# Key tiles of the second block's attention: two heads in one tile, 64-row scores, meta parts multiplied together

## The reference

```python
# windowed attention: 16 query heads, 4 key heads of 64; 256 keys under a mask, 16 meta keys, a sink
s_band = where(mask, q @ k.T * 64 ** -0.5, -1e30)
s_meta = q @ k_meta.T * 64 ** -0.5
p = softmax(concat([s_band, s_meta, sink]))
o = p_band @ v + p_meta @ v_meta
# differential attention: 8 heads, two key and query parts of 64 each, values of 128, all 272 keys
p = softmax(q_c @ k_c.T * 64 ** -0.5)          # c = 0, 1
o = rms_norm((p_0 - lam * p_1) @ v) * (1 - lambda_init)
```

## Time and profile before

| what | value |
|---|---|
| median of 3 runs | 981.12 us |
| lowest, highest | 980.5, 982.21 us |
| span of the profiled execution (its own time, first to last instruction) | 978.5 us |
| mean granted TensorE clock in it | 0.990 |
| PE busy | 952.4 us (97%) |
| weight loads busy | 846.0 us (86%) |
| DVE, ACT, POOL busy | 591.6, 451.9, 47.2 us |

### The profile page before, as it was taken

One profiled execution on the slowest core, in us unless ns is written; L12 is line 12 of the kernel. 1 busy time (PEld: TensorE's weight loads), 2 busy tenths in 40 slices (PEclk: granted clock), 3 DMA queues, 4 the chain that ended last, 5 costly groups with the idle time before them and its releaser, 6 DMA issues.

```text
span 978.5 us, 15576 instructions
## 1 busy us (share of the span) xinstructions
PE 952.4 (97%) x6056; PEld 846.0 (86%) x6056; DVE 591.6 (60%) x1088; ACT 451.9 (46%) x752; POOL 47.2 (5%) x92
## 2 busy tenths in 40 slices
PE   6999999999999999979999999999999899999997
PEld 4888999987999999857778889999999699999996
DVE  5666765566545544577745776577766664554454
ACT  6535535345544344344444454556543454434432
POOL 0000010000000000020000000022230100000000
PEclk7999999999999999989999999999999999999999
DMA  9653334553555454513332212222245355545531
GB/s 349 245 213 134 125 130 172 173 206 130 209 178 201 176 177 157 181 44 129 150 137 101 86 45 86 87 87 87 92 160 223 130 176 192 191 171 184 201 130 44
DMA packets 21541, 148.94 MB, mean 152 GB/s; under 512 B 2528, under 2 KB 2784, under 8 KB 3952
## 3 DMA queue, kind: packets, MB, share of 16 engines
q1 hardware_dynamic: 20592, 145.52, 41.8%
q10 hardware_dynamic: 896, 2.69, 0.8%
HBM read 147.15 MB, written 1.05 MB: 151 GB/s over the span
## 4 chain that ended last, share of the span: by engine, by line
PE 93%; DVE 3%; ACT 1%; POOL 1%; issue 1%; DMA 1%; POOLq 0%; SPq 0%; ACTq 0%; DVEq 0%
PE ps L385 26%; PE ps L386 26%; PE ps L387 26%; PE ps L1252 3%; PE ps L1203 2%; PE ps L1223 2%; PE ps L1205 1%; PE ps L1254 1%; PE ps L394 1%; DVE xT_l L1366 1%; PE ps L1209 1%; PE ps L1210 1%; PE ps L397 1%; PE ps L961 1%; POOL stat L902 1%; DVE xn L1359 1%
## 5 line engine op out<-in xcount | busy, mean ns | idle before, releaser
L1345 DVE TENSOR_TENSOR wlo<-raw,whi 128x2048 fp32r<-128x2048 f32 x135 | 308.8, 2290 | 216.4 <-ACT whi L510 216.1
L510 ACT ACTIVATE whi<-raw 128x2048 fp32r<-128x2048 f32 x135 | 258.2, 1917 | 243.8 <-PE ps L387 232.5
L385 PE MATMUL ps<-xT_h,whi 128*128 128x256 f32 x864 | 246.5, 285 | 1.5 <-DVE xT_l L1366 1.5
L386 PE MATMUL ps<-xT_l,whi 128*128 128x256 f32 x864 | 244.4, 283 | 0.0
L387 PE MATMUL ps<-xT_h,wlo 128*128 128x256 f32 x864 | 244.3, 283 | 0.0
L385 PEld LDWEIGHTS ps<-xT_h,whi 128*128 128x128 f32 x864 | 165.5, 192 | 2.6 <-issue 1.9
L386 PEld LDWEIGHTS ps<-xT_l,whi 128*128 128x128 f32 x864 | 165.5, 192 | 0.6
L387 PEld LDWEIGHTS ps<-xT_h,wlo 128*128 128x128 f32 x864 | 165.5, 192 | 0.0
L385 PE MATMUL ps<-whi,xT_h 128*128 128x512 f32 (+1 forms) x336 | 133.8, 398 | 3.1 <-DVE xT_l L1366 3.1
L387 PE MATMUL ps<-whi,xT_l 128*128 128x512 f32 (+1 forms) x336 | 130.8, 389 | 0.0
L386 PE MATMUL ps<-wlo,xT_h 128*128 128x512 f32 (+1 forms) x336 | 130.7, 389 | 0.0
(11 more groups left out here) (296 smaller groups left out, 1392.4 us busy)
## 6 DMA issues: line engine op xcount, KB each, us to landing
raw<-weights SPq DMA_DIRECT2D x135, 1024.0 KB, 4.8
cst<-consts SPq DMA_DIRECT2D x1, 1571.0 KB, 13.5
h<-x_tiles SPq DMA_DIRECT2D x2, 512.0 KB, 5.5
raw<-weights SPq DMA_DIRECT2D x2, 512.0 KB, 6.7
gain_rows<-gain_rows ACTq DMA_DIRECT2D x1, 1024.0 KB, 7.1
y<-h ACTq DMA_DIRECT2D x4, 256.0 KB, 2.3
gain_row<-gain_rows ACTq DMA_DIRECT2D x1, 512.0 KB, 3.8
row<-rows SPq DMA_DIRECT2D x1, 144.0 KB, 14.4
```

The source lines that it names most:

```text
L385: pe.matmul(o, lh, rh, start=first, stop=False)
L386: pe.matmul(o, lh, rl, start=False, stop=False)
L510: act.activation(whi[s][:], raw[s][:], ACT.Copy).then_inc(split_hi, 1)
L1345: dve.tensor_tensor(wlo[s][:], raw[s][:], whi[s][:], ALU.subtract).then_inc(split_lo, 1)
```

## The change

Keys: `ksT` and `kbT` hold the two heads of a pair on partitions 0 to 63 and 64 to 127 of one tile, without zeros; ACT writes them with fewer copies (for `kbT` one of 128 partitions in place of two of 64; for `ksT` three per pair in place of two). In `ksT` the second head's keys stand with the 16 meta keys first. Scores: one product per head over all 272 keys, from the 64 rows of that head, into bank 4 (first head) and bank 5 (second). DVE takes one reduction of 272 per head; the maximum over two parts goes, and the constants gain 48 columns of zeros around the mask. The probabilities of both heads lie in one tile so that their meta parts are 16 columns, a gap of 16 zeros, and 16 columns; one transpose turns both. The meta values become tiles of 128 partitions, zero but for partitions 0 to 15 and 32 to 47, and one 128-row product opens the accumulation for both heads. POOL clears these value tiles, the gaps and `pmT`, and no longer the key tiles.

```diff
-        kbT = new("kbT", [P, 2 * F_HEADS, KEYS])
-        ksT = new("ksT", [P, S_KV, KEYS])
-        vs_meta = new("vs_meta", [N_META, S_KV * DH])
+        kbT = new("kbT", [P, F_HEADS, KEYS])
+        ksT = new("ksT", [P, S_KV // 2, KEYS])
+        vs_meta = new("vs_meta", [P, S_KV * DH])
...
-        sc = [new("sc0", [P, 2, KEYS]), new("sc1", [P, 2, KEYS])]
+        sc = [new("sc0", [P, SECOND + KEYS]), new("sc1", [P, SECOND + KEYS])]    # SECOND = 256 + 32
...
-        pmT = new("pmT", [N_META, 2, P])
+        pmT = new("pmT", [P, P])
...
-                        ins = copy_halves(*((ksT, 2 * cc) if r == 0 else (kbT, 4 * (r - 1) + 2 * cc)), 4 + cc)
+                        if r == 0:
+                            act.activation(ksT[0:DH, cc, :], ps[0:DH, 4 + cc, 0:KEYS], ACT.Copy)
+                            act.activation(ksT[DH:P, cc, N_META:KEYS], ps[DH:P, 4 + cc, 0:TOK], ACT.Copy)
+                            ins = act.activation(ksT[DH:P, cc, 0:N_META], ps[DH:P, 4 + cc, TOK:KEYS], ACT.Copy)
+                        else:
+                            ins = act.activation(kbT[:, 2 * (r - 1) + cc, :], ps[:, 4 + cc, 0:KEYS], ACT.Copy)
...
-            pool.memset(ksT[:], 0.0)
-            pool.memset(kbT[:], 0.0).then_inc(zero2, 1)
+            pool.memset(vs_meta[:], 0.0)
+            pool.memset(vb_meta[:], 0.0)
+            for b in range(2):
+                pool.memset(sc[b][:, KEYS:SECOND], 0.0)
+            pool.memset(pmT[:], 0.0).then_inc(zero2, 1)
...
                     if U < S_UNITS:
+                        pe.matmul(o, pmT[:], vs_meta[:, cc // 4 * P:(cc // 4 + 1) * P], start=True, stop=False)
                         for u in range(2):
                             a = (2 * (cc // 4) + u) * DH
                             for kt in range(NT):
-                                pe.matmul(o[:, u * DH:(u + 1) * DH], puT[:, 2 * u + kt, :], vs[:, kt, a:a + DH],
-                                          start=kt == 0, stop=False)
-                            m = pe.matmul(o[:, u * DH:(u + 1) * DH], pmT[:, u, :], vs_meta[:, a:a + DH],
-                                          start=False, stop=True)
+                                m = pe.matmul(o[:, u * DH:(u + 1) * DH], puT[:, 2 * u + kt, :], vs[:, kt, a:a + DH],
+                                              start=False, stop=u + kt == 2)
                     else:
+                        pe.matmul(o, pmT[:], vb_meta[:, cc * P:(cc + 1) * P], start=True, stop=False)
                         for kt in range(NT):
-                            pe.matmul(o, puT[:, kt, :], vb[:, kt, cc * P:(cc + 1) * P], start=kt == 0, stop=False)
-                        m = pe.matmul(o, pmT[:, 0, :], vb_meta[:, cc * P:(cc + 1) * P], start=False, stop=True)
+                            m = pe.matmul(o, puT[:, kt, :], vb[:, kt, cc * P:(cc + 1) * P], start=False, stop=kt == 1)
...
-                    for u in range(heads):
-                        m = pe.transpose(ps[0:N_META, 7, 32 + u * P:32 + (u + 1) * P], sc[U % 2][:, u, TOK:KEYS],
-                                         ident)
-                    m.then_inc(u_pt, 1)
+                    both = SECOND + N_META if heads == 2 else SECOND
+                    pe.transpose(ps[0:both - TOK, 7, 32:32 + P], sc[U % 2][:, TOK:both], ident).then_inc(u_pt, 1)
...
                     for u in range(2):
-                        kT = ksT[:, 2 * (cc // 4) + u, :] if U < S_UNITS else kbT[:, 2 * cc + u, :]
-                        pe.matmul(ps[:, 4, u * TOK:(u + 1) * TOK], qT[:, cc, t * P:(t + 1) * P], kT[:, 0:TOK],
-                                  start=True, stop=True)
-                        m = pe.matmul(ps[:, 5, u * N_META:(u + 1) * N_META], qT[:, cc, t * P:(t + 1) * P],
-                                      kT[:, TOK:KEYS], start=True, stop=True)
+                        half = slice(u * DH, (u + 1) * DH)
+                        kT = ksT[half, cc // 4, :] if U < S_UNITS else kbT[half, cc, :]
+                        m = pe.matmul(ps[:, 4 + u, 0:KEYS], qT[half, cc, t * P:(t + 1) * P], kT, start=True, stop=True)
...
                 for u in range(2):
-                    for part, (src, a, b) in enumerate(((ps[:, 4, u * TOK:(u + 1) * TOK], 0, TOK),
-                                                        (ps[:, 5, u * N_META:(u + 1) * N_META], TOK, KEYS))):
...
+                    src, o = ps[:, 4 + u, 0:KEYS], scores(U, u)
...
-                link(dve, "dve", dve.tensor_tensor(st[:, 0, :], st[:, 0, :], st[:, 1, :], ALU.max))
...
-                                meta_sum(vs_meta[:], 6, 256, 512)
+                                dve.wait_ge(zero2, 1)
+                                for u in range(2):
+                                    meta_sum_heads(vs_meta[u * QUAD:u * QUAD + N_META, :], u)
```

More of the change, by code:

```diff
@@ L43 @@
 KEYS = TOK + N_META
+QUAD = 32
+SECOND = TOK + QUAD
 MIX1 = 2 + 1 + 2 + 2 + 4 + 4 + 4 + 4 + 2 + 4 + 4
@@ L157, in c, with scores, scores_of_tile @@
             return cst[:, a:a + n]
+        def scores(U, u):
+            return sc[U % 2][:, u * SECOND:u * SECOND + KEYS]
+        def scores_of_tile(U, u, kt):
+            a = kt * P + (SECOND + N_META if u else 0)
+            return sc[U % 2][:, a:a + P]
         def cl(name, i=0, n=1):
@@ L759, in _ @@
                     act.wait_ge(u_pt, U + 1)
-                    heads = 2 if U < S_UNITS else 1
-                    act.activation(pmT[:, 0:heads, :], ps[0:N_META, 7, 32:32 + heads * P].rearrange(
-                        "p (a q) -> p a q", a=heads), ACT.Copy).then_inc(u_ptm, 1)
+                    rows_used = QUAD + N_META if U < S_UNITS else QUAD
+                    act.activation(pmT[0:rows_used, :], ps[0:rows_used, 7, 32:32 + P], ACT.Copy).then_inc(u_ptm, 1)
                 U = q - U0 - 4
@@ L785, in _ @@
                     act.activation((sT_h if U < S_UNITS else dT_h)[:, U % S_UNITS // 2, U % 2 * P:(U % 2 + 1) * P],
-                                   ps[:, 5, P:2 * P], ACT.Copy,
+                                   ps[:, 5, 3 * P:4 * P], ACT.Copy,
                                    scale=1.0 if U < S_UNITS else subgain[:]).then_inc(d_hi, 1)
@@ L795, in _ @@
                     for u in range(2):
-                        ins = act.activation(sc[U % 2][:, u, :], sc[U % 2][:, u, :], ACT.Exp,
+                        ins = act.activation(scores(U, u), scores(U, u), ACT.Exp,
                                              bias=st[:, 2, u:u + 1], accum_out=st[:, 4, u:u + 1])
@@ L1511, in unit_front @@
                     dve.wait_ge(u_pt, U - 1)
[L1512 to L1517, removed]
-                for u in range(2):
-                    for part, (src, a, b) in enumerate(((ps[:, 4, u * TOK:(u + 1) * TOK], 0, TOK),
-                                                        (ps[:, 5, u * N_META:(u + 1) * N_META], TOK, KEYS))):
[L1521 to L1532, removed]
+                st = usoft[:, U % 4]
+                for u in range(2):
+                    src, o = ps[:, 4 + u, 0:KEYS], scores(U, u)
+                    if U < S_UNITS:
+                        a = CONST["ge" if U % 2 else "zero"][0] + (0 if U % 2 else N_META) - u * N_META
+                        mask = cst[:, a:a + KEYS]
+                    else:
+                        mask = c("zero")[:, 0:KEYS // 2].unsqueeze(1).to_broadcast([P, 2, KEYS // 2])
+                        src, o = (v.rearrange("p (a k) -> p a k", a=2) for v in (src, o))
+                    m = dve.tensor_tensor_reduce(out=o, in0=src, in1=mask, scale=DH ** -0.5, scalar=NEG,
+                                                 op0=ALU.add, op1=ALU.max, accum_out=st[:, 0, u:u + 1])
                 link(dve, "dve", m)
-                link(dve, "dve", dve.tensor_tensor(st[:, 0, :], st[:, 0, :], st[:, 1, :], ALU.max))
                 if U < S_UNITS:
@@ L1552, in unit_back @@
                     dve.tensor_tensor(st[:, 5, 1:2], st[:, 5, 1:2], neglam[:], ALU.mult)
-                    link(dve, "dve", dve.tensor_scalar(s[:, 0, :], s[:, 0, :], st[:, 5, 0:1], None, ALU.mult))
-                    ins = dve.scalar_tensor_tensor(out=s[:, 0, :], in0=s[:, 1, :], scalar=st[:, 5, 1:2],
-                                                   in1=s[:, 0, :], op0=ALU.mult, op1=ALU.add)
+                    first, second = scores(U, 0), scores(U, 1)
+                    link(dve, "dve", dve.tensor_scalar(first, first, st[:, 5, 0:1], None, ALU.mult))
+                    ins = dve.scalar_tensor_tensor(out=first, in0=second, scalar=st[:, 5, 1:2],
+                                                   in1=first, op0=ALU.mult, op1=ALU.add)
                 ins.then_inc(u_pr, 1)
@@ L1738, in _ @@
                     dve.wait_ge(mlow_ok, 4 + half)
-                    meta_free(meta_sum(vb_meta[:, half * BANK:(half + 1) * BANK], 7 - half, 0, BANK))
+                    meta_free(meta_sum(vb_meta[0:N_META, half * BANK:(half + 1) * BANK], 7 - half, 0, BANK))
                 U = q - U0 - 3
```

21 lines of the change are left out of this document (11 added, 10 removed).

## The result

The changed kernel takes 945.14 us (median of 4 runs, 944.03 to 946.69), the kernel before 980.89 us beside it (980.5 to 982.21). The ratio is 0.9633, with a 95% interval of 0.9621 to 0.9646: 35.8 us or 3.7% faster. The forecast was 948.7 us. The profiled execution is the slowest of the four runs, 946.69 us with a span of 944.9.

A forecast was written before the change was run, and what follows sets the result against it. PE was taken to bound the kernel, busy 97% of the span. Savings of 13.8 + 5.6 + 8.6 + 2.9 + 1.5 = 32.4 us gave a span of 946.1 and a time of 948.7 us, range 943.5 to 961.

The forecast's parts named there:

- Values: Value products and transposes: fewer loads and no change of rows save 13.8 us in windowed units, 5.6 in differential ones.
- Scores: Score products of all 32 units: four loads and passes on 64 rows replace eight loads, saving 8.6 us.
- n = 3: Four score passes cost three pass times, the middle two running together: 1.04 us a unit; chance 0.50.
- n = 2: Four score passes cost two pass times, 0.81 us a unit: the lower end of the scores' price.
- The entry: Going from 128 rows to 64 before the scores: a pause of 0.15 us a unit.
- leaving: Going back from 64 rows after the last score pass: 0.09 us of emptying a unit.
- full overlap: Rival: the heads' score passes overlap fully, 941.3 us; chance 0.07 together with no emptying around 64 rows.
- in a line: Rival: the four score passes run one behind the other, scores save 1.3 us, time 956.0 us; chance 0.32.
- Clearing: POOL's five shorter clearings before the first blob let DVE finish earlier, so the blob starts 2.9 us earlier.
- Clock: Behind the first blob: with PE's wait gone the granted clock stays up, 1.5 us saved, bounds 0 and 1.8.

The follow-up runs named there:

- e3: Changed kernel with the joint meta product taken from the 48 rows that hold data in place of 128: 958.27 us.
- e4: Changed kernel with the joint 128-column meta product done as two of 64 columns in the windowed units: 949.35 us.
- e1: Changed kernel with both heads' scores taken from the same rows, partitions 0 to 63: 960.6 us.
- e6: Changed kernel with POOL waiting with its clearings until DVE's normalisation is done: 944.97 us.
- e7: Changed kernel with the first half's features copied out before the second half is normalised, whose transposes move into the first half's blobs: 940.72 us.
- e2: Changed kernel with both heads' scores taken from all 128 rows over 272 keys: 947.04 us.
- e5: Changed kernel with POOL also clearing the key tiles ahead of its own five clearings: 946.23 us.

## Why the prediction was right, and where it was not

**Values.** 13.8 and 5.6 us forecast, 14.2 and 5.4 measured. The loads follow each other at 0.11, without a pause, as said; each head was priced at 0.95 where the first took 1.07, and the ten loads at 1.10 where they took 1.18, which nearly cancel. e3 and e4 show both reasons, the missing change of rows and the missing loads.

**Scores.** 8.6 forecast, 14.4 measured. The step that failed is "PE's order (both passes of head 0, then both of head 1) lets the second pass of the first head and the first of the second head run together: n = 3". PE starts the two heads' first passes together, although the program names the second head's product after that of the first, so n = 2. (The trace doesn't name the head of a pass; that the two of a pair are of different heads follows from e1, where products on the same rows never pair.) The entry was dearer than said, 0.20 in place of 0.15, and leaving was 0.09 as said (0.66 less a load of 0.11 and two passes of 0.23). That is the rival "full overlap" by its mechanism, which had a chance of 0.07 together with another; e1 shows that different rows are what it needs, and that in a line nothing would have been gained.

**Clearing.** 2.9 forecast, 3.0 measured. DVE waited for all five clearings, as in the sum. That it would gain nothing by getting in earlier came true as well: e6 shows it.

**Clock.** 1.5 forecast, nothing measured in the profiled execution: the stretch behind the first blob takes 84.10 us, 84.02 before. The step that failed is "With the wait gone PE is idle for well under a microsecond". PE still waits for ACT's and DVE's copies around the first blob (1.79 us busy of the 3.50 from 426.5 to 430), and the clock fell again. The price itself was right: where the clock stayed up at 430 (e1, e3 to e6) that stretch took 82.5 us, 1.6 less. PE is as idle there in e1, e3 and e4 (1.76 to 1.79 us busy in the same 3.50), so the one profiled execution doesn't settle whether the clock falls there: of the seven of the changed kernel and e1 to e6, it fell there in two.

**Sum.** With the sizes measured: 14.2 + 5.4 + 14.4 + 3.0 = 37.0 us, against 32.4 forecast. The two executions differ by 33.6. Of the 3.4 between, 1.5 is the clock's fall at 235.5 in the first block, which the execution before doesn't have. Another 1.0 builds up in the first block in small steps, 0.7 in the last stretch, and 0.1 lies in the blobs. The 1.0 and the 0.7 belong to the change: the first block shows 1.04 to 1.07 in the eight executions of changed kernels (without the first 32 us and the falls), and the last stretch 0.7 in each of the four without a fall at 750 (after, e1, e3 and e7). The prediction had this at nothing. Most of it is the pace of products whose code isn't edited: behind the units 183 steps between products of `dT` take 22.03 us after (696.78 to 718.81) and 21.55 before (731.14 to 752.69), both at full clock and without a gap, and `retT` and `aT` of the first block go from 0.117 to 0.120 us a product. All these tiles lie behind the constants, which the change made 48 columns wider, so they moved; `xT`, which lies ahead of them, has 0.120 in both. Whether the place is the cause no run shows.

So the time fell inside the forecast range with one term sized 5.8 us too small, one 1.5 too large, and 3.2 us outside the edited code against them. Luck has a part in this: the mechanism that came true was priced at 941.3, outside the range, and was brought back in by the dearer entry (0.05 x 32 = 1.6), the clock term and those 3.2 us. The medians differ by more than the two executions, 35.8, since the profiled one after is the slowest of its four (1.6 above the median) and the one before a quick one (its span with the 1.8 that lie between span and time in the other runs is 980.3, 0.6 below the median).

## What to carry to other kernels

Price a change of a product's rows as an item of its own: here 0.38 to 0.39 us for one visit to fewer rows and back, which is more than three weight loads, so zeros in unused rows are cheaper than fewer rows. Splitting the rows between two products pays only if the two run at once and are long enough for that to outweigh the emptyings; here that left 0.05 us a unit, and folding short products into long ones earned the rest. Where one engine's long write holds up another's instruction on the way to the next product, ask which write the instruction really waits for, and what else is late by then.

## What was not expected of the hardware

Two fp32 products of two passes each, on rows 0 to 63 and 64 to 127, ran pass against pass, 0.01 us apart, in all 32 units, not one product after the other as the program names them.

The clock's falls at the three pauses for the block norms (about 235, 420 to 430 and 750 us) come and go from one execution to the next, with the same code ahead of them: at 430 the clock fell in the profiled executions of after and e2 and not in those of e1 and e3 to e6 (in e5 it fell at 420.7 instead), at 750 in those of e2 and e4 to e6 alone. One fall costs 1.5 to 2.7 us in its stretch (84.0 against 82.5; 244.2 and 245.4 against 242.7). This is about the scatter of the runs, and a forecast that counts on one such fall being there or not is worth no more than its chance.
